# Products of the unit matrix issued in TensorE's long waits, into the bank that is written next

## Chip, cores and metric

One core of one Trainium2 chip. The metric is the device time of one execution in microseconds; lower is better.

## What is computed

Three blocks follow one another on an activation of 1024 tokens x 1024 channels, all in float32. Cut to what shapes the kernel:

```python
def first_block(x, ...):        # an even layer, an odd layer, rmsnorm
    # even: p = rmsnorm(h, g) @ w_in; an RWKV recurrence over tokens (8 heads of 64) and a banded
    #       softmax attention (8 heads) side by side; both gated; h + concat(y_a, y_b) @ w_out
    # odd:  p = rmsnorm(h, g) @ w_in; spatial gating: per 128 tokens and group, sg_w @ layernorm(v);
    #       h + (y * silu(gate)) @ w_out
def second_block(x, ...):       # one norm, one wide projection, three branches, merged
    # sliding-window attention with sinks, a 31-tap conv with layernorm, differential attention;
    # each branch through its w_o and a sigmoid merge gate; the sum @ w_out
def third_block(x, p, ...):
    # x = layer_norm(x); stick-breaking attention and a multiscale pool; @ w_out; layer_norm
    # h = square(relu(x @ w_up)) @ w_down; layer_norm;  x + (p @ w_ple) * sigmoid(x @ w_ple_gate); layer_norm
def step(state, inp):           # the recurrence inside the even layer
    r_t, w_t, k_t, v_t, a_t, b_t = inp
    sa = jnp.einsum('bhvk,bhk->bhv', state, a_t)
    state = state * w_t[:, :, None, :] + sa[..., None] * b_t[:, :, None, :] + v_t[..., None] * k_t[:, :, None, :]
    return state, jnp.einsum('bhvk,bhk->bhv', state, r_t)
```

## The kernel before

Each engine has one program, written out by hand in its final order; nothing is scheduled or reordered by a tool. The engines meet only through semaphores: `done(name)` gives the semaphore and the count at which a named step is finished, and an engine waits for it before it issues what needs it. So TensorE works through one fixed list, and whatever stands behind a waiting product waits too.

The results of products go to the eight PSUM banks. A ring (`Banks`) hands them out in turn. `open` takes the next bank, and `free` names the step that emptied it the last time round, which the program waits for first; the waits for the operands come behind that one.

The stages, in order: the first norm (`begin`); the RWKV branch (`pe_rwkv`) paced step by step against the banded attention (`pe_band`), 280 rounds of one against 192 of the other; the even layer's gate and output (`pe_even`); the odd layer (`pe_odd`); the projections of the second block, with head sums `hn` for its q and k norms, and the window attention (`pe_window`); the joins, the differential attention, the merge (`pe_merged`); the third block's attention (`pe_stick`), its output product (`pe_outp`), the MLP (`pe_mlp`) and the last gate.

The RWKV branch runs over four pairs of heads (c = 0 to 3). After the projections come transposes of v (`v_tr`), then four groups of 2 x 128 tokens. In `pe_factor` a group's triangular inverse is built by doubling: for i = 1 to 5 a product `ym` (four of 128x128), one `f` and one `g`, each emptied by VectorE or ScalarE before the next can start. Ahead of the first `ym` VectorE masks the scores and forms `Fm` and `Gm` (L2321 to L2332). The state steps of the group before (`pe_chunks`) and the band's products are woven between. At the end of a head pair VectorE normalises y in a row of 128x1024 operations (up to L2312), and then TensorE transposes it (`y_tr`).

At the end of a layer the tiles of 128 tokens are normalised one after another, and TensorE transposes each for the next stage (`pe_rms_tile`, `pe_ln_tile`, tile `tr`). `follow` issues a tile's transposes a few tiles of products later, so that the last tiles have no products left to stand between them. In the third block GpSimd ends each tile's norm (L3115).

`ident` is the 128x128 unit matrix in float32, made at the start. A float32 product leaves two records in the profile (one for each of its two passes), a product of float32r operands or a transpose leaves one.

Of the kernel before, what the change touches and what calls it, by code (L numbers as in the profile page):

```python
# [13 lines left out]
P = 128  # L14
# [154 lines left out]
def build(nc, T, out):  # L169
    ctx = ExitStack()  # L170
    with ctx:
# [15 lines left out]
        ident = sb("ident", [P, P])  # L187
# [82 lines left out]
        E = V = S = G = Y = Dry()  # L270
# [50 lines left out]
        def by4(b):  # L321
            return b.rearrange("p (b m n) -> p b m n", b=4, m=2)
# [7 lines left out]
        def gn(b):  # L330
# [2 lines left out]
        idb = ident[:, :].unsqueeze(1).to_broadcast([P, 4, P])  # L333
        handed = [(A[:, 768:1024], SIG[:, 256:512], by4(CS), by4(EX)),
                  (SIG[:, 512:768], SIG[:, 768:1024], by4(WS0[:, 3072:4096]), by4(WS1[:, 3072:4096]))]
        SM, SV = STAT[:, 48:64], STAT[:, 64:80]
        w_rw, w_band = slot(WS0, KD, 3 * P), slot(WS1, KD, 3 * P)
        w_lora = slot(WS0, KD, P, 3072)
# [150 lines left out]
                                                            4864)  # L489


        def pe_product_T(st, R_, name, wv, src, kt, c0, *waits):
            for half in range(2):
                b = R_.open(st.name, *name, half)
                pe.wait_ge(*R_.free(st.name, *name, half))
                for w in waits:
                    pe.wait_ge(*w)
                for k in range(kt):
                    mm = E.matmul(b[:, :], wv[:, k, c0:c0 + P], src[:, k, half * HALF:(half + 1) * HALF],  # L499
                                  start=k == 0, stop=k == kt - 1)  # L500
                mm.then_inc(*st.pe.mark(st.name, *name, half))
                yield
# [11 lines left out]
        def pe_transposes(st, R_, name, srcs, *waits):  # L514
            b = R_.open(st.name, *name)
            pe.wait_ge(*R_.free(st.name, *name))
            pe.wait_ge(*done("consts"))
            for w in waits:
                pe.wait_ge(*w)
            for i, s in enumerate(srcs):  # L520
                mm = E.transpose(b[:, i * P:(i + 1) * P], s, ident[:, :])  # L521
            mm.then_inc(*st.pe.mark(st.name, *name))

        def pe_split(st, R_, name, n, kt, left, right, *waits):
            b = R_.open(st.name, *name)
            pe.wait_ge(*R_.free(st.name, *name))
            for w in waits:
                pe.wait_ge(*w)
            ks = range(kt) if isinstance(kt, int) else kt
            for k in ks:  # L530
                (lh, ll), (rh, rl) = left(k), right(k)
                E.matmul(b[:, 0:n], lh, rh, start=k == ks[0], stop=False)  # L532
                E.matmul(b[:, 0:n], lh, rl, start=False, stop=False)  # L533
                mm = E.matmul(b[:, 0:n], ll, rh, start=False, stop=k == ks[-1])  # L534
            mm.then_inc(*st.pe.mark(st.name, *name))
# [42 lines left out]
        def pe_rwkv():  # L578
            after(pe, begin)
            run(pe_product_T(rw, for_rw, ("lora",), w_lora, XT, KD, 0, done("rwkv", "w_lora")))  # L580
            for c in range(4):
# [3 lines left out]
                for hf in range(2):  # L585
                    sl = slice(hf * HALF, (hf + 1) * HALF)
                    for lo, what in ((0, "sig"), (64, "a")):
                        b = for_rw.open("rwkv", what, c, hf)
                        pe.wait_ge(*for_rw.free("rwkv", what, c, hf))
                        pe.wait_ge(*done("rwkv", "lora_ready"))  # L590
                        pe.wait_ge(*done("rwkv", "w_lora2"))
                        E.matmul(b[:, :], W2[lo:lo + 64, c * P:(c + 1) * P], LT[lo:lo + 64, sl], start=True,
                                 stop=True).then_inc(*rw.pe.mark("rwkv", what, c, hf))
# [44 lines left out]
        def pe_factor(c, grp):  # L638
# [20 lines left out]
            for i in range(1, 6):  # L659
                yield  # L660
                b = for_rw.open("rwkv", "ym", c, grp, i)
                pe.wait_ge(*for_rw.free("rwkv", "ym", c, grp, i))
                pe.wait_ge(*done("rwkv", "al", c, grp, i))
                pe.wait_ge(*done("rwkv", "fg", c, grp, i - 1))
                for q in range(4):
# [37 lines left out]
            for i in range(2):  # L703
                t = 2 * grp + i
# [106 lines left out]
        def pe_odd():  # L811
# [11 lines left out]
            def mixed(t):  # L823
                yield from nothing(4)
                for hf in range(2):
                    b = every.open("odd", "mix", t, hf)
                    pe.wait_ge(*every.free("odd", "mix", t, hf))
                    pe.wait_ge(*done("odd", "vn", t))
                    pe.wait_ge(*done("odd", "sgt"))
                    for g in range(4):  # L830
                        gg = hf * 4 + g
                        mm = E.matmul(b[:, g * P:(g + 1) * P], VN_O[:, t, gg * P:(gg + 1) * P], SGT[:, gg, :],
                                      start=True, stop=True)
                    mm.then_inc(*odd.pe.mark("odd", "mix", t, hf))
                yield
# [34 lines left out]
        def pe_head_sums(st, areas, order, k):  # L870

            name = order[k]
            b = every.open(st.name, "hn", *name)
            pe.wait_ge(*every.free(st.name, "hn", *name))
            pe.wait_ge(*done(st.name, "sq", *name))
            E.matmul(b[:, :], head_ones[:, :], areas[k % 2][1], start=True, stop=True).then_inc(
                *st.pe.mark(st.name, "hn", *name))
# [2696 lines left out]
```

## Time and profile before

| | |
|---|---|
| median of 3 runs | 4776.83 us (4765.28 to 4786.88) |
| the profiled execution | 4775.21 us, span 4773.1 us, mean granted TensorE clock 0.931 |
| TensorE busy | 4285.7 us (90% of the span), 21360 records |
| VectorE, ScalarE, GpSimd busy | 1861.4, 1319.7, 1121.0 us |
| DMA | 35 GB/s over the span, q1 at 10.7% of its engines |

All times are from the start of the span. A busy share is that of an engine's own instructions; the granted clock of a stretch is the mean of two levels, 2.4 GHz (1.0) and 1.2 GHz (0.5). An "idle before" is the time in which the engine stood still just ahead of a row, with the instruction that ended it.

### The profile page before, as it was taken

What the parts mean: (1) busy time and instruction counts of PE and PEld (TensorE: products, weight loads), DVE (VectorE), ACT (ScalarE), POOL (GpSimd) and SP (SyncE); (2) the same over time, 40 slices, a digit from 0 to 9 for tenths busy, and PEclk for the clock granted to TensorE, in tenths of its full rate; (3) what the DMA queues carried; (4) which work ended last, traced back from release to release, by engine and by line L of the source; (5) the groups of instructions that cost most, each with busy time, mean ns of one, the idle gap of its engine ahead of it and who ended that gap; (6) DMA issues with size and microseconds to landing.
All of it is one profiled execution on the core that took longest, in us unless ns stands there. A gap on an engine that the chain in (4) does not pass through costs nothing.

```text
span 4773.1 us, 50138 instructions
## 1 busy us (share of the span) xinstructions
PE 4285.7 (90%) x21360; PEld 3309.7 (69%) x21360; DVE 1861.4 (39%) x3046; ACT 1319.7 (28%) x2333; POOL 1121.0 (23%) x579
## 2 busy tenths in 40 slices
PE   8888888888978999988799997998998989999988
PEld 4775756757548889766667775776447768888877
DVE  2444425434222312685520358222137332333243
ACT  3222222222112322444321236211137222111223
POOL 1101101101111143674322210223000043232343
PEclk9999898898989999998899988999998889999989
DMA  2101000000021111210011110121100011111110
GB/s 79 27 1 28 1 15 14 1 15 1 5 98 36 36 53 36 80 40 18 18 36 40 49 36 1 51 73 47 35 18 1 27 62 44 53 45 53 45 53 36
DMA packets 155582, 168.08 MB, mean 35 GB/s; under 512 B 8032, under 2 KB 137952, under 8 KB 155360
## 3 DMA queue, kind: packets, MB, share of 16 engines
q1 hardware_dynamic: 155360, 164.89, 10.7%
q8 instruction: 168, 2.75, 0.2%
q14 instruction: 54, 0.44, 0.0%
HBM read 156.48 MB, written 8.39 MB: 35 GB/s over the span
## 4 chain that ended last, share of the span: by engine, by line
PE 41%; DVE 5%; ACT 2%; POOL 1%; issue 1%; DMA 0%; POOLq 0%; ACTq 0%; DVEq 0%
PE bank L532 9%; PE bank L533 9%; PE bank L534 9%; PE bank L510 4%; PE bank L499 3%; PE bank L977 2%; PE bank L521 1%; PE bank L995 1%; PE bank L1142 1%; PE bank L1118 1%; POOL H L3113 0%; POOL H L3115 0%; PE bank L1025 0%; DVE BIG L2743 0%; DVE BIG L2806 0%
## 5 line engine op out<-in xcount | busy, mean ns | idle before, releaser
L532 PE MATMUL bank<-XT_r,W_r 128*128 128x512 f32 x1712 | 701.2, 410 | 11.0 <-POOL BIG_r L3216 8.2
L533 PE MATMUL bank<-BIG_r,W_r 128*128 128x512 f32 x1712 | 677.5, 396 | 0.0
L499 PE MATMUL bank<-XT,W 128*128 128x512 f32 x1312 | 584.1, 603 | 20.5 <-DMA W<-w_in_e 17.8
L499 PEld LDWEIGHTS bank<-XT,W 128*128 128x128 f32 x1312 | 250.9, 194 | 330.1 <-issue 321.0
L534 PE MATMUL bank<-XT_r,W_r 128*128 128x512 f32 x1200 | 475.5, 396 | 0.0
L532 PE MATMUL bank<-W_r,BIG_r 128*128 128x256 f32 (+1 forms) x1280 | 419.1, 327 | 9.0 <-DVE MIX_r L2472 4.5
L3068 POOL TENSOR_TENSOR W_r<-W,W_r 128x2048 fp32r<-128x2048 f32 (+1 forms) x64 | 260.8, 4075 | 612.2 <-ACT W_r L1263 612.2
L532 PEld LDWEIGHTS bank<-XT_r,W_r 128*128 128x128 f32 x1712 | 329.4, 192 | 91.2 <-issue 21.3
L533 PEld LDWEIGHTS bank<-BIG_r,W_r 128*128 128x128 f32 x1712 | 329.1, 192 | 78.0 <-issue 11.3
L534 PE MATMUL bank<-W_r,BIG_r 128*128 128x256 f32 (+1 forms) x1152 | 381.2, 331 | 0.0
L1253 ACT ACTIVATE BIG<-bank 128x512 f32<-128x512 f32 (+3 forms) x246 | 130.0, 537 | 494.6 <-PE bank L499 153.6
L534 PEld LDWEIGHTS bank<-XT_r,W_r 128*128 128x128 f32 x1200 | 231.4, 193 | 50.0
L532 PEld LDWEIGHTS bank<-W_r,BIG_r 128*128 128x128 f32 x1280 | 244.5, 191 | 31.0 <-ACT BIG_r L1596 4.9
L521 PE MATMUL bank<-ident,BIG 128*128 128x128 f32 x688 | 133.7, 344 | 136.5 <-ACT BIG L1253 51.3
L3216 POOL TENSOR_TENSOR BIG_r<-MIX,W_r 128x2048 fp32r<-128x2048 f32 x36 | 165.4, 4596 | 329.8 <-ACT W_r L1927 329.8
L534 PEld LDWEIGHTS bank<-W_r,BIG_r 128*128 128x128 f32 x1152 | 219.6, 191 | 20.0
L521 PEld LDWEIGHTS bank<-ident,BIG 128*128 128x128 f32 x688 | 100.1, 177 | 177.6 <-ACT BIG L1253 70.8
L533 PE MATMUL bank<-W_r,BIG_r 128*128 128x256 f32 x768 | 218.2, 284 | 0.0
L534 PE MATMUL bank<-W_r,MIX_r 128*128 128x256 f32 x768 | 218.2, 284 | 0.0
L3113 POOL TENSOR_TENSOR H<-H,BIG 128x1024 f32<-128x1024 f32 x32 | 75.8, 2367 | 600.9 <-ACT H L1370 600.9
L2870 DVE TENSOR_TENSOR H<-H,bank 128x512 f32<-128x512 f32 x240 | 161.7, 686 | 121.0 <-PE bank L534 121.0
L534 PE MATMUL bank<-XT_r,BIG_r 128*128 128x512 f32 x512 | 200.1, 391 | 0.0
(391 smaller groups left out, 7912.3 us busy)
## 6 DMA issues: line engine op xcount, KB each, us to landing
W<-w_in SPq DMA_DIRECT2D x22, 1024.0 KB, 5.3
MIX<-w_up SPq DMA_DIRECT2D x16, 1024.0 KB, 5.4
MIX<-w_down SPq DMA_DIRECT2D x16, 1024.0 KB, 4.8
W<-w_in_e SPq DMA_DIRECT2D x26, 512.0 KB, 6.5
W<-w_in_o SPq DMA_DIRECT2D x12, 1024.0 KB, 5.1
W<-w_in SPq DMA_DIRECT2D x17, 512.0 KB, 4.0
H<-x SPq DMA_DIRECT2D x16, 512.0 KB, 7.7
W<-w_out SPq DMA_DIRECT2D x8, 1024.0 KB, 5.2
```

Source lines behind the costliest of these rows:

```text
L499: mm = E.matmul(b[:, :], wv[:, k, c0:c0 + P], src[:, k, half * HALF:(half + 1) * HALF], start=k == 0, stop=k == kt - 1)
L510: mm = E.matmul(b[:, 0:n], src[:, k, t * P:(t + 1) * P], wv[:, k, c0:c0 + n], start=k == 0, stop=k == kt - 1)
L521: mm = E.transpose(b[:, i * P:(i + 1) * P], s, ident[:, :])
L532: E.matmul(b[:, 0:n], lh, rh, start=k == ks[0], stop=False)
L533: E.matmul(b[:, 0:n], lh, rl, start=False, stop=False)
L534: mm = E.matmul(b[:, 0:n], ll, rh, start=False, stop=k == ks[-1])
L977: mm = E.matmul(b[:, :], wo[:, k, :], half_of(Yb[:, k, :], half), start=k == 0, stop=k == 3)
L1253: S.activation(dst, R_.bank(st.name, *name)[:, 0:width], ACT.Copy, scale=scale).then_inc(*st.act.mark("ev", st.name, *name))
L2870: V.tensor_tensor(h, h, b, ALU.add).then_inc(*ff.dve.mark("ev", "mlp", "down", n, t, c0))
L3068: G.tensor_tensor(WLO[k % 2][:, 0:n], WSTAGE[k % 2][:, 0:n], WHI[k % 2][:, 0:n], ALU.subtract).then_inc(*s_split.mark("split", k))
L3113: G.tensor_tensor(x, x, ROWS[:, 0:D], ALU.mult).then_inc(*st.pool.mark())
L3216: G.tensor_tensor(WL[k % 2][:, :], STAGE[k % 2], WH[k % 2][:, :], ALU.subtract).then_inc(*st.pool.mark(st.name, "split", k))
```

## The change

A table `KEEP_UP` names 52 places in TensorE's program, each by the bank that it opens, and gives a number of products, 699 in all. At such a place `pe_keep_up` issues that many products of the unit matrix with itself, 128x128 in float32, into columns 0 to 127 of the bank that has just been opened. It stands behind the wait for the bank and ahead of the waits for the operands. The real product starts with `start=True` and overwrites what they left. The products signal nothing, no other engine's program changes, and no wait is added.

The places: ahead of the first gate product on the low-rank path (`sig`), the transposes of v (4) and of y (4), and the first `ym` of 15 of the 16 groups, all in the RWKV branch; the even gate; tiles at the ends of the even, odd, merge, output and MLP stages (18); three `mix` products and the first output product of the odd layer; four head sums; and the MLP's first product.

```diff
--- before.py
+++ after.py
@@ -333,6 +333,16 @@
         idb = ident[:, :].unsqueeze(1).to_broadcast([P, 4, P])
         handed = [(A[:, 768:1024], SIG[:, 256:512], by4(CS), by4(EX)),
                   (SIG[:, 512:768], SIG[:, 768:1024], by4(WS0[:, 3072:4096]), by4(WS1[:, 3072:4096]))]
+        KEEP_UP = {("rwkv", "sig", 0, 0): 18, ("even", "gate", 0, 0): 48, ("odd", "out", 0, 0): 15,
+                   ("mlp", "up", 0, 0, 0): 28, ("odd", "mix", 4, 0): 8, ("odd", "mix", 5, 0): 12, ("odd", "mix", 6, 0): 7,
+                   ("window", "hn", "q", 1, 0): 21, ("window", "hn", "q", 2, 1): 15, ("window", "hn", "q", 3, 1): 4,
+                   ("window", "hn", "k", 1, 1): 7}
+        KEEP_UP.update({("rwkv", "v_tr", c, 0): 14 for c in range(4)})
+        KEEP_UP.update({("rwkv", "y_tr", c, 0): n for c, n in enumerate((10, 38, 38, 42))})
+        KEEP_UP.update({("rwkv", "ym", c, grp, 1): 8 for c in range(4) for grp in range(4) if c or grp})
+        for st_, ts in (("even", {5: 15, 6: 15, 7: 5}), ("odd", {2: 7, 3: 4, 4: 15}), ("merged", {4: 17, 5: 9, 6: 9, 7: 9}),
+                        ("outp", {5: 22, 6: 14, 7: 14}), ("mlp", {0: 7, 4: 12, 5: 10, 6: 14, 7: 14})):
+            KEEP_UP.update({(st_, "tr", t, 0): n for t, n in ts.items()})
         SM, SV = STAT[:, 48:64], STAT[:, 64:80]
         w_rw, w_band = slot(WS0, KD, 3 * P), slot(WS1, KD, 3 * P)
         w_lora = slot(WS0, KD, P, 3072)
@@ -489,10 +499,16 @@
                                                             4864)
 
 
+        def pe_keep_up(b, *name):
+
+            for _ in range(KEEP_UP.get(name, 0)):
+                E.matmul(b[:, 0:P], ident[:, :], ident[:, :], start=True, stop=True)
+
         def pe_product_T(st, R_, name, wv, src, kt, c0, *waits):
             for half in range(2):
                 b = R_.open(st.name, *name, half)
                 pe.wait_ge(*R_.free(st.name, *name, half))
+                pe_keep_up(b, st.name, *name, half)
                 for w in waits:
                     pe.wait_ge(*w)
                 for k in range(kt):
@@ -515,6 +531,7 @@
             b = R_.open(st.name, *name)
             pe.wait_ge(*R_.free(st.name, *name))
             pe.wait_ge(*done("consts"))
+            pe_keep_up(b, st.name, *name)
             for w in waits:
                 pe.wait_ge(*w)
             for i, s in enumerate(srcs):
@@ -524,6 +541,7 @@
         def pe_split(st, R_, name, n, kt, left, right, *waits):
             b = R_.open(st.name, *name)
             pe.wait_ge(*R_.free(st.name, *name))
+            pe_keep_up(b, st.name, *name)
             for w in waits:
                 pe.wait_ge(*w)
             ks = range(kt) if isinstance(kt, int) else kt
@@ -587,6 +605,7 @@
                     for lo, what in ((0, "sig"), (64, "a")):
                         b = for_rw.open("rwkv", what, c, hf)
                         pe.wait_ge(*for_rw.free("rwkv", what, c, hf))
+                        pe_keep_up(b, "rwkv", what, c, hf)
                         pe.wait_ge(*done("rwkv", "lora_ready"))
                         pe.wait_ge(*done("rwkv", "w_lora2"))
                         E.matmul(b[:, :], W2[lo:lo + 64, c * P:(c + 1) * P], LT[lo:lo + 64, sl], start=True,
@@ -660,6 +679,7 @@
                 yield
                 b = for_rw.open("rwkv", "ym", c, grp, i)
                 pe.wait_ge(*for_rw.free("rwkv", "ym", c, grp, i))
+                pe_keep_up(b, "rwkv", "ym", c, grp, i)
                 pe.wait_ge(*done("rwkv", "al", c, grp, i))
                 pe.wait_ge(*done("rwkv", "fg", c, grp, i - 1))
                 for q in range(4):
@@ -825,6 +845,7 @@
                 for hf in range(2):
                     b = every.open("odd", "mix", t, hf)
                     pe.wait_ge(*every.free("odd", "mix", t, hf))
+                    pe_keep_up(b, "odd", "mix", t, hf)
                     pe.wait_ge(*done("odd", "vn", t))
                     pe.wait_ge(*done("odd", "sgt"))
                     for g in range(4):
@@ -872,6 +893,7 @@
             name = order[k]
             b = every.open(st.name, "hn", *name)
             pe.wait_ge(*every.free(st.name, "hn", *name))
+            pe_keep_up(b, st.name, "hn", *name)
             pe.wait_ge(*done(st.name, "sq", *name))
             E.matmul(b[:, :], head_ones[:, :], areas[k % 2][1], start=True, stop=True).then_inc(
                 *st.pe.mark(st.name, "hn", *name))
```

TensorE's list at the end of head pair c = 1 of the RWKV branch, before. L742/L743 and L769 are the last state step and band scores, L521 the transposes (`ident,MIX` is `y_tr`), L592 the low-rank products of the next head pair:

```order
512 L769 MATMUL bank<-H 128x128
513 L521 MATMUL bank<-ident,H 128x128
514 L521 MATMUL bank<-ident,MIX 128x128 x8
515 L592 MATMUL bank<-BIG 128x512 x4
516 L499 MATMUL bank<-XT,W 128x512 x8
```

The same place now; L505 is the product in `pe_keep_up`:

```order
523 L789 MATMUL bank<-H 128x128
524 L538 MATMUL bank<-ident,H 128x128
525 L505 MATMUL bank<-ident 128x128 x38
526 L538 MATMUL bank<-ident,MIX 128x128 x8
527 L611 MATMUL bank<-BIG 128x512 x4
528 L515 MATMUL bank<-XT,W 128x512 x8
```

Thirty-eight products stand between the band's last transpose and `y_tr`; the order of the rest is as it was.

TensorE's list ahead of a group's first `ym` (c = 2, third group). L725 and L729 are state products (L745 and L749 now), L667 is `ym` (L687 now), L734 and L736 (L754 and L756) the next state step, L675 (L695) the `f` product. Before:

```order
629 L725 MATMUL bank<-BIG 128x128
630 L729 MATMUL bank<-BIG 128x128
631 L667 MATMUL bank<-BIG 128x128 x4
632 L521 MATMUL bank<-ident,H 128x128 x5
633 L734 MATMUL bank<-BIG 128x128
```

And now:

```order
644 L745 MATMUL bank<-BIG 128x128
645 L749 MATMUL bank<-BIG 128x128
646 L505 MATMUL bank<-ident 128x128 x8
647 L687 MATMUL bank<-BIG 128x128 x4
648 L538 MATMUL bank<-ident,H 128x128 x5
649 L754 MATMUL bank<-BIG 128x128
```

Eight products stand ahead of `ym`, behind the state products.

## Rows read from the trace of the kernel before

**Rows 1.** The profile's page: span, busy time, granted clock in 40 slices

```profile
span 4773.1 us, 50138 instructions
...
PE 4285.7 (90%) x21360; PEld 3309.7 (69%) x21360; DVE 1861.4 (39%) x3046; ACT 1319.7 (28%) x2333; POOL 1121.0 (23%) x579
...
PEclk9999898898989999998899988999998889999989
```

**Rows 2.** 70 half-rate stretches (window, length, busy by engine, clock, DMA)

```profile
22.50:29.30 6.80, 5.82 (x24) 4.71 (x24) 4.08 (x10) 3.85 (x7) 0.00 (x0) 0.50 1.04 257
...
sum 664.10, PE 489.31 PEld 389.08 DVE 325.68 ACT 227.78 POOL 146.12; mean PE 6.99 PEld 5.56 DVE 4.65 ACT 3.25 POOL 2.09
```

**Rows 3.** Two like steps of the RWKV chain as windows

```profile
808.72:822.65 13.93, 13.93 (x57) 12.43 (x57) 4.40 (x10) 2.28 (x5) 1.55 (x2) 0.50 0.00 1
829.00:837.19 8.19, 7.21 (x51) 6.00 (x51) 4.87 (x11) 2.56 (x6) 1.27 (x1) 1.00 0.00 0
```

**Rows 4.** TensorE's waits (us in total, times, longest)

```profile
PE bank L667 <- DVE BIG L2332: 40.4, 15, 3.9
```

**Rows 5.** TensorE in order of time (start, us, instructions, [idle before <-releaser])

```profile
277.84 1.13 PE L667 MATMUL bank<-BIG 128*128 128x128 f32 x8 [1.02 <-DVE BIG L2332]
...
669.79 5.30 PE L510 MATMUL bank<-W,XT 128*128 128x128 f32 x46
...
674.92 0.39 PE L725 MATMUL bank<-BIG 128*128 128x128 f32 x2
...
690.37 1.97 PE L521 MATMUL bank<-ident,MIX 128*128 128x128 f32 x8 [11.08 <-DVE MIX L2312]
...
750.83 3.65 PE L521 MATMUL bank<-ident,BIG 128*128 128x128 f32 x16 [4.08 <-DVE BIG L2222]
...
862.79 1.62 PE L667 MATMUL bank<-BIG 128*128 128x128 f32 x6 [3.09 <-DVE BIG L2332]
...
1352.47 23.12 PE L499 MATMUL bank<-XT,W 128*128 128x512 f32 x48 [14.63 <-DMA W<-w_in_e]
```

**Rows 6.** 128x128 products back to back at half rate, TensorE in order of time

```profile
810.59 1.92 PE L682 MATMUL bank<-BIG 128*128 128x128 f32 x8
...
812.29 1.81 PE L783 MATMUL bank<-H 128*128 128x64 f32 x8
```

**Rows 7.** TensorE's ladder of transposes at the output stage's end

```profile
3871.70 1.94 PE L521 MATMUL bank<-ident,H 128*128 128x128 f32 x8 [6.44 <-DVE STAT L2151]
3883.98 1.94 PE L521 MATMUL bank<-ident,H 128*128 128x128 f32 x8 [4.26 <-POOL H L3115]
3894.09 0.76 PE L532 MATMUL bank<-XT_r,W_r 128*128 128x512 f32 x1 [8.17 <-POOL BIG_r L3216]
```

**Rows 8.** Half-rate stretches of the RWKV stage after filled waits, 21 windows: sum

```profile
sum 155.90, PE 148.63 PEld 126.82 DVE 54.14 ACT 38.24 POOL 19.99; mean PE 7.08 PEld 6.04 DVE 2.58 ACT 1.82 POOL 0.95
```

**Rows 9.** Half-rate stretches of the later stages after filled waits, 11 windows: sum

```profile
sum 54.10, PE 49.88 PEld 40.18 DVE 22.72 ACT 15.18 POOL 21.40; mean PE 4.53 PEld 3.65 DVE 2.07 ACT 1.38 POOL 1.95
```

**Rows 10.** Six of these stretches (452.9, 690.4, 1012.7, 1090.8, 1352.5, 3894.1): sum

```profile
sum 38.20, PE 36.54 PEld 26.00 DVE 5.72 ACT 9.79 POOL 8.98; mean PE 6.09 PEld 4.33 DVE 0.95 ACT 1.63 POOL 1.50
```

**Rows 11.** Four of them, after ladders (1525.0, 3300.3, 3894.1, 4623.6): sum

```profile
sum 28.20, PE 24.03 PEld 20.11 DVE 5.97 ACT 5.98 POOL 10.93; mean PE 6.01 PEld 5.03 DVE 1.49 ACT 1.49 POOL 2.73
```

**Rows 12.** Two waits and the clock behind them

```profile
368.87 1.10 PE L521 MATMUL bank<-ident,MIX 128*128 128x128 f32 x8 [3.01 <-DVE MIX L2312]
...
490.08 1.19 PE L667 MATMUL bank<-BIG 128*128 128x128 f32 x4 [1.66 <-DVE BIG L2332]
...
365.00:375.00 10.00, 6.16 (x25) 2.63 (x24) 4.44 (x5) 4.90 (x7) 0.00 (x0) 1.00 0.09 15
490.10:496.90 6.80, 6.80 (x29) 6.35 (x30) 2.43 (x7) 1.47 (x4) 1.27 (x1) 0.50 0.01 2
```

**Rows 13.** TensorE's first transposes

```profile
15.24 1.97 PE L521 MATMUL bank<-ident,BIG 128*128 128x128 f32 x8 [0.55 <-ACT BIG L1310]
20.36 1.06 PE L521 MATMUL bank<-ident,BIG 128*128 128x128 f32 x8 [0.90 <-DVE STAT L2048]
```

## Prediction

> **What bounds the kernel now.** I read the page first [rows 1]. TensorE is busy 90% of the span, no other engine above 39%, and the granted clock dips in many of the 40 slices. TensorE sets the time, then, and it is slowed in two ways: it waits, and for a while after some waits it runs at half rate. The second view is a table of the stretches in which the granted clock is 0.50, the lower level of 1.2 GHz. There are 70, of 664.1 us together, with TensorE busy for 489.3 us of them [rows 2]. The rest of the span runs at 1.0, 2.4 GHz.
>
> What does a half-rate stretch cost? The third view sets two like steps of the RWKV chain side by side, from one `f` product to the next [rows 3]. At 1.0 the step took 8.19 us for 51 records, at 0.50 it took 13.93 us for 57. By the columns of their products the two hold nearly the same work. So the slow one pays 5.74 us, 0.41 of its busy time. Nothing hid it: VectorE's and TensorE's parts alternate, and each product that lasts longer moves the whole chain. If I scale by records (8.19 x 57 / 51 = 9.15), it pays 4.8 us, or 0.34. If everything merely halved, it would be 0.50. I take 0.41, and keep the other two for the range.
>
> The waits that go before are in the waits view and in the order of time: the first `ym` of a group behind VectorE's masks (L2332, 40.4 us in 15 waits) [rows 4], `y_tr` 11.08 us, `v_tr` 4.08, the even gate 14.63 behind its weights' DMA [rows 5], the output stage's ladder 6.44, 4.26 and 8.17 [rows 7].
>
> **The change: what the products cost.** A 128x128 float32 product is two records. Back to back at full clock, 46 records took 674.92 - 669.79 = 5.13 us, so 0.112 each and 0.223 us for a product [rows 5]. At half rate 8 records took 812.29 - 810.59 = 1.70 us, 0.425 us for a product [rows 6]. So 699 products are 156 us of TensorE at full clock, and whether they cost anything is a question of room. The waits have it: 38 products before `y_tr` are 8.5 us in a wait of 11.08; 14 before `v_tr` 3.1 in 4.08; 8 before `ym` 1.8 in 3.09; 48 before the even gate 10.7 in 14.63 [rows 5]; 22 and 14 in the ladder 4.9 and 3.1 in 6.44 and 4.26; 28 before the MLP 6.3 in 8.17 [rows 7]. All end about 1 us or more before the operands come. I find one place without room, the `ym` that waited 1.02 us (1.8 us of products, 0.8 us late) [rows 5]. The wait that covers them belongs to VectorE, ScalarE, GpSimd or a DMA, and none of these has a new instruction or a new wait. The bank is waited for first, but it was free at or before the end of the previous product nearly everywhere, since a ring of four or eight banks lies between. Queued behind the products stand only the product that waits anyway and what follows it. If the cover were gone, the cost would be the 156 us.
>
> **What they give.** The change can touch only the falls of the clock that follow one of its 52 places. I took each half-rate stretch of that kind, from the moment when the operands came to its end. What lies earlier is waiting, which a faster clock does not shorten. In the RWKV stage these are 21 stretches with 148.6 us of busy time [rows 8], later 11 with 49.9 us [rows 9]. Together 198.5 us, and at 0.41 that is 82 us if every such fall goes away; 67 us at 0.34, 99 at 0.50.
>
> Not all of them will go. The products end early, and the rest of the wait stays idle. The trace has a fall straight after a wait of 1.66 us, and none after one of 3.01 us [rows 12], so the length of a wait alone does not decide, and a rest of 1 us may or may not be harmless. Two classes follow. Where more than about 2 us stay idle I count the fall as kept: two `y_tr` (11.08 - 8.5 = 2.6), the even gate (3.9), the MLP's first product (1.9), and the two `ym` whose waits are longest (3.9 us in [rows 4], less 1.8). By the same windows these six hold 36.5 us of busy time [rows 10], so 15 us. Of the other 67 us I take one in five as kept, since the chain behind `ym` has idle time of its own in every step (8.19 less 7.21 us busy in the fast one [rows 3]): 13 us. And where the clock is already low as the products begin, they run at 0.425 and come late: 14 before `v_tr` take 6.0 us for 4.08, 1.9 late. One or two such places and the short `ym` make 3 us.
>
> Sum: 82 - 15 - 13 - 3 = 51 us. From the profiled execution's 4775.2 us that is 4724. The median of the three runs is 1.6 us above this execution, so 4726.
>
> The 38 half-rate stretches that remain (window and differential attention, the stick-breaking rounds, the band's steps) have no products before them and stay as they are.
>
> **A rule against the change.** TensorE's first instructions are transposes, products against the unit matrix. Eight took 1.97 us at 15.24 and, with nothing but transposes in between, 1.06 us at 20.36 [rows 13]: the clock rose while only they ran. The Trainium skill (TensorE: Matmul & The Clock Gate, Part 4: PE-mode transpose) says the full clock does not engage for transpose-mode, which is not counted as busy in the same way. Here the trace disagrees. By that rule the ladders, where only transposes stand between the filled waits, would keep their falls.
>
> **Rivals.**
> *Falls kept in the ladders.* If what stands between the waits does too little, the ladders of the even, merge, output and MLP stages keep their falls. Their part is 24.0 us of busy time [rows 11], 10 us at 0.41; 5.9 of it (the MLP's first product) is already counted as kept. So 7 us less gain, 4733. The first transposes speak against it. It lies inside my range and goes with the forecast.
>
> *Half of the falls stay.* The idle rests of 1.0 to 1.5 us are enough together with the chain's own idle time. The gain is 82 / 2 = 41, less the 15 that are kept in any case and some 6 us of late operands: 20 us, 4756. The fall after 1.66 us speaks for it, the full clock after 3.01 us against.
>
> *The products don't hold the clock at all, and make operands' consumers late: slower.* The unit matrix with itself is mostly zeros, and no row shows a product of just that kind. If the clock falls where it did, the rest of the products runs at 0.425. All of them at that rate would overrun their waits by 5.1 us at each of two `y_tr` (38 x 0.425 - 11.08), 5.8 at the gate (20.4 - 14.63), 3.7 at the MLP (11.9 - 8.17), 1.9 at a `v_tr`, 0.3 at a `ym` [rows 5, 7], some 80 us over the 52 places. About the first 2 us of each wait still pass at full clock, which takes off nearly 0.9 us a place: 35 us remain, 4811. It decides once the lateness passes what the prevented falls give back. The first transposes speak against it, since they too are products with the unit matrix.
>
> *Every fall goes:* 82 us, 4694.
>
> **How the numbers follow.** Forecast with its ladder variant, 4705 to 4751: 0.64. Half or more stay, 4751 to 4775: 0.20. Nearly all go, below 4705: 0.10. Products that don't hold the clock: 0.05. No effect either way: 0.01. The range leaves out the slow rival, the best of the full gain at 0.50, and the weakest part of the second: 4694 to 4759. From no change a measurement of this kernel tells about 0.5%, 24 us. Gains under 24 us have most of the second case: faster 0.79, same 0.16, slower 0.05.
>
> **What would show it.** TensorE's records rise by 1398 to 22758. The sum of half-rate stretches falls from 664 us to under 350, and the mean granted clock rises from 0.931 to about 0.97. Before `y_tr` and `ym` a block of products ends 1 us or more before the operand's row, and the idle time there shrinks to the rest. The steps behind `ym` take some 8 us in place of 14. Wrong would be: half-rate stretches that begin inside the blocks of products, or rows that now follow such a block without idle time, at twice the price; or waits of TensorE that grow elsewhere by what the RWKV chain gained.

## The result and the profile after

The changed kernel took 4727.11 us (median of 4 runs, 4725.53 to 4728.78) against 4777.45 us (4765.28 to 4786.88) before: a ratio of 0.9896, 95% interval 0.9873 to 0.9919. It is faster by 50 us, 1.0%. The forecast was 4726.0.

The page of the kernel after, its lines on the span, on TensorE and on the granted clock, which answer to [rows 1]:

```profile
span 4723.6 us, 52912 instructions
...
PE 4374.3 (93%) x22758; PEld 3410.2 (72%) x22758; DVE 1859.8 (39%) x3046; ACT 1317.7 (28%) x2333; POOL 1120.0 (24%) x579
...
PEclk9998999999999999998899988999998899999999
```

TensorE has 1398 more records and is busy for 88.6 us more, and yet the span is shorter. The mean granted clock rose from 0.931 to 0.959. (The record of the clock begins with its first rise, at 19.0 us before and 24.0 us after; what lies ahead of it is counted as full.) The half-rate stretches as windows, after (the first two of 55 and their sum; columns as in [rows 2]):

```profile
303.90:324.40 20.50, 18.18 (x67) 14.25 (x65) 5.00 (x15) 3.15 (x8) 0.00 (x0) 0.50 0.00 1
430.20:437.00 6.80, 5.79 (x30) 5.49 (x32) 3.48 (x7) 2.24 (x6) 0.22 (x1) 0.50 0.00 0
...
sum 390.70, PE 332.89 PEld 258.71 DVE 175.58 ACT 136.59 POOL 64.20; mean PE 6.05 PEld 4.70 DVE 3.19 ACT 2.48 POOL 1.17
```

Seventy stretches of 664.1 us [rows 2] became 55 of 390.7 us. The product itself and TensorE's two great waits of [rows 4, 7], now; the first line is from the groups, the two others from the waits:

```profile
L505 PE MATMUL bank<-ident 128*128 128x128 f32 x1398 | 169.6, 280 | 2.8 <-DVE BIG_r L2185 1.7 <-ACT MIX L1275 0.9
```

```profile
PE bank L538 <- POOL H L3137: 21.7, 16, 1.9
...
PE bank L687 <- DVE BIG L2354: 13.5, 13, 2.2
```

`ym`'s wait for the masks fell from 40.4 us with 3.9 at most to 13.5 with 2.2 at most. What the waits look like from inside is in TensorE's order of time. First `y_tr` of c = 1 (in [rows 5] the row with 11.08 us of idle time), then one step of the chain at c = 2 (as in [rows 3]), then `y_tr` of c = 3 and the even gate:

```profile
664.49 8.65 PE L505 MATMUL bank<-ident 128*128 128x128 f32 x76
675.72 1.78 PE L538 MATMUL bank<-ident,MIX 128*128 128x128 f32 x8 [2.58 <-DVE MIX L2334]
...
833.73 2.05 PE L505 MATMUL bank<-ident 128*128 128x128 f32 x16
836.95 1.13 PE L687 MATMUL bank<-BIG 128*128 128x128 f32 x8 [1.17 <-DVE BIG L2354]
...
839.19 1.16 PE L695 MATMUL bank<-BIG 128*128 128x128 f32 x8
...
847.01 1.13 PE L695 MATMUL bank<-BIG 128*128 128x128 f32 x8
...
1284.32 10.86 PE L505 MATMUL bank<-ident 128*128 128x128 f32 x84
1296.96 1.09 PE L538 MATMUL bank<-ident,MIX 128*128 128x128 f32 x8 [1.78 <-DVE MIX L2334]
1298.99 10.96 PE L505 MATMUL bank<-ident 128*128 128x128 f32 x96 [0.94 <-ACT MIX L1275]
1313.09 5.40 PE L515 MATMUL bank<-XT,W 128*128 128x512 f32 x8 [3.15 <-DMA W<-w_in_e]
```

The reader is to see three things. The 76 records before `y_tr` end 2.58 us ahead of the operand, and behind that rest the eight transposes take 1.78 us: this fall stayed. The 16 before `ym` end 1.17 us ahead, `ym` takes 1.13 us, and the step from one `f` to the next takes 847.01 - 839.19 = 7.82 us. And before the gate 3.15 us stay idle, behind which the clock fell too.

Where the time came from, by stages. Each ends with the first record of the product named, and half-rate us stand in brackets; both are worked out from the traces. The rows together are the whole span. The last three columns belong to the last experiments.

| stage up to | before | after | spare bank | more covered | both |
|---|---|---|---|---|---|
| `v_tr` c = 0 | 129.6 (15.0) | 126.6 (0) | 127.2 (6.8) | 127.3 (6.8) | 127.9 (6.8) |
| `v_tr` c = 1 | 308.6 (43.0) | 298.7 (20.5) | 298.5 (20.5) | 291.7 (3.4) | 292.5 (3.4) |
| `v_tr` c = 2 | 312.6 (66.2) | 310.3 (44.4) | 309.7 (44.4) | 296.8 (10.2) | 297.7 (13.7) |
| `v_tr` c = 3 | 321.7 (84.0) | 301.0 (23.9) | 300.9 (23.9) | 300.4 (23.9) | 300.4 (23.9) |
| even gate | 279.9 (80.7) | 276.6 (37.5) | 279.5 (44.4) | 270.8 (23.9) | 271.6 (23.9) |
| odd layer's first transposes | 176.1 (19.0) | 175.3 (6.8) | 172.2 (0) | 172.2 (0) | 172.4 (0) |
| odd layer's first output product | 301.5 (14.8) | 299.3 (3.4) | 300.2 (6.8) | 297.8 (0) | 299.2 (3.4) |
| second block's projections | 122.3 (8.3) | 118.3 (0) | 118.7 (0) | 118.2 (0) | 118.4 (0) |
| window attention's first scores (projections, head sums) | 192.3 (10.2) | 192.5 (3.4) | 192.5 (0.2) | 192.5 (0) | 192.6 (2.1) |
| joins (the window attention) | 235.4 (70.6) | 235.2 (70.6) | 220.5 (19.2) | 235.0 (70.6) | 215.8 (14.4) |
| third block's output product | 1366.4 (175.1) | 1366.7 (151.5) | 1366.5 (151.3) | 1369.9 (171.8) | 1365.8 (150.7) |
| MLP's first product | 147.7 (28.3) | 147.7 (6.6) | 148.0 (6.8) | 146.7 (6.7) | 146.8 (6.9) |
| last gate | 733.1 (26.5) | 729.6 (0.3) | 729.6 (0.4) | 729.7 (0) | 729.6 (0) |
| end | 146.0 (19.7) | 145.8 (19.6) | 145.8 (19.5) | 145.8 (18.8) | 145.9 (18.7) |

Up to the even gate the kernel before needs 1352.5 us and the changed one 1313.1: 39.4 of the 49.5 us by which the spans differ. All that follows gives 10.

### The profile page after: what moved, and what is told of

Its sections match the earlier page's. It is cut to its first block, busy times and chain, and to the rows that moved or that the text cites. A ratio compares the mean times of both kernels' runs of the same rounds, so it can differ in the third digit from the quotient of the medians.

```text
span 4723.6 us, 52912 instructions
## 1 busy us (share of the span) xinstructions
PE 4374.3 (93%) x22758; PEld 3410.2 (72%) x22758; DVE 1859.8 (39%) x3046; ACT 1317.7 (28%) x2333; POOL 1120.0 (24%) x579
## 4 chain that ended last, share of the span: by engine, by line
PE 42%; DVE 5%; ACT 2%; POOL 1%; issue 1%; DMA 0%; POOLq 0%; ACTq 0%; DVEq 0%
PE bank L550 9%; PE bank L551 9%; PE bank L552 9%; PE bank L526 4%; PE bank L515 4%; PE bank L999 2%; PE bank L1017 1%; PE bank L538 1%; PE bank L1140 1%; PE bank L1164 1%; POOL H L3135 0%; POOL H L3137 0%; PE bank L1047 0%; DVE BIG L2828 0%; DVE BIG L2765 0%
## 5 line engine op out<-in xcount | busy, mean ns | idle before, releaser
L515 PE MATMUL bank<-XT,W 128*128 128x512 f32 x1312 | 582.2, 602 | 10.2 <-DMA W<-w_in_e 6.5
L1275 ACT ACTIVATE BIG<-bank 128x512 f32<-128x512 f32 (+3 forms) x246 | 129.9, 536 | 489.9 <-PE bank L515 153.5
L550 PEld LDWEIGHTS bank<-W_r,BIG_r 128*128 128x128 f32 x1280 | 244.1, 191 | 27.3 <-issue 4.0
L551 PE MATMUL bank<-BIG_r 128*128 128x512 f32 x512 | 199.2, 389 | 0.0
```

Of the source, the lines that this page charges most:

```text
L1275: S.activation(dst, R_.bank(st.name, *name)[:, 0:width], ACT.Copy, scale=scale).then_inc(*st.act.mark("ev", st.name, *name))
```

## The experiments

Theory A in the expectations is the prediction's own: the products keep the clock up, and a fall costs 0.41 of TensorE's busy time in it, wherever it lies. The rivals stand beside it in each expectation. All kernels compute the whole output. The edits are to the changed kernel.

**Only the RWKV places.**

```diff
+        KEEP_UP = {k: n for k, n in KEEP_UP.items() if k[0] == "rwkv"}
```

> Only the 24 places of the RWKV branch keep their products (322 of 699). Theory A (the gain is the higher clock behind the waits, in proportion to the busy time of the half-rate stretches that vanish): the changed kernel left TensorE's `even gate` 39.4 us earlier and gave 50.3 us in all, so this version gains 38 to 40 us, 4738, about 0.992 of the kernel before. Theory B (a cost of about 1 us for the first product after every long wait, whatever the clock, which any product in the wait takes away): 24 of 52 places give 23 us, 4754, 0.995.

Measured: 4732.16 us, ratio 0.9911 (0.9898 to 0.9924), a gain of 44 us with 322 of the 699 products. Theory B of the expectation (a cost of 1 us for each long wait, whatever the clock) had 23 us.

**Only the later places.**

```diff
+        KEEP_UP = {k: n for k, n in KEEP_UP.items() if k[0] != "rwkv"}
```

> Only the 28 places outside the RWKV branch keep their products (377 of 699). Theory A (clock): 10 to 12 us of gain, 4766, 0.9977, since most of these places stand in ladders of transposes that wait for another engine anyway. Theory B (a cost of each long wait): 28 of 52 places give 27 us, 4750, 0.994. By either theory the gains of this version and of the RWKV-only one add up to 50 us.

Measured: 4772.61 us (4764.54 to 4781.29), ratio 0.9991 (0.9983 to 1.0), a gain of 4 us with 377 products. The gain goes neither by the number of products nor by that of waits (theory B had 27 us here), and both parts together make 48 of the 50 us. In this version's profile the stages behind the even gate without the window attention give 10.3 us, in the changed kernel 10.0, but the window attention, which the edit doesn't touch, took 6.0 us more than before. Much of the half-rate time that vanished in the later stages gave nothing, and the output stage's ladder shows why. TensorE's order of time in the changed kernel, where [rows 7] were:

```profile
3825.29 1.09 PE L538 MATMUL bank<-ident,H 128*128 128x128 f32 x8 [1.45 <-POOL H L3137]
3826.22 3.29 PE L505 MATMUL bank<-ident 128*128 128x128 f32 x28
3831.43 1.09 PE L538 MATMUL bank<-ident,H 128*128 128x128 f32 x8 [1.93 <-POOL H L3137]
3832.36 3.29 PE L505 MATMUL bank<-ident 128*128 128x128 f32 x28
3837.58 1.09 PE L538 MATMUL bank<-ident,H 128*128 128x128 f32 x8 [1.93 <-POOL H L3137]
3840.34 8.01 PE L505 MATMUL bank<-ident 128*128 128x128 f32 x56 [1.67 <-DVE BIG_r L2185]
3848.11 0.48 PE L550 MATMUL bank<-XT_r,W_r 128*128 128x512 f32 x1
```

The transposes take 1.09 us in place of 1.94, so the clock stayed up. But a tile follows the one before it after 6.14 and 6.15 us, and before the two steps from 3871.70 to 3883.98 [rows 7] took 12.28 us, 6.14 each on average. The tiles come at the pace at which their norm is made, and a slow transpose between two waits costs nothing. That is the stage in which the half-rate time fell by 21.7 us and the span not at all. Before the MLP's first product the block began at 3840.34 behind 1.67 us of idle time, in which the clock had just fallen (at 3840.1). So its 56 records took 8.01 us (at 0.112 each 6.3), and the product follows it without a rest, 10.53 us after the start of the last tile's transposes in place of 10.11 [rows 7]: late by 0.4 us or more.

**Transposes in place of products.** Two for each product, so that the number of records stays.

```diff
-            for _ in range(KEEP_UP.get(name, 0)):
-                E.matmul(b[:, 0:P], ident[:, :], ident[:, :], start=True, stop=True)
+            for _ in range(2 * KEEP_UP.get(name, 0)):
+                E.transpose(b[:, 0:P], ident[:, :], ident[:, :])
```

> The same 52 places, but each product of the unit matrix is replaced by two transposes of it, so that the number of records and their time stay. If transposes hold the clock as products do, as TensorE's first transposes suggested: 4727, 0.990, half-rate stretches of about 390 us together. If transposes are not counted as work (the rule of the Trainium skill, TensorE: Matmul & The Clock Gate, Part 4: PE-mode transpose): the falls come back, 664 us at half rate, no gain, and late operands on top, 4777 to 4811, 1.000 to 1.007.

Measured: 4721.51 us, ratio 0.9887 (0.9874 to 0.99), with 56 half-rate stretches of 390.8 us and a mean clock of 0.959. The block before `y_tr` of c = 1, TensorE in order of time:

```profile
660.53 8.46 PE L505 MATMUL bank<-ident 128*128 128x128 f32 x76
671.76 1.30 PE L538 MATMUL bank<-ident,MIX 128*128 128x128 f32 x8 [2.77 <-DVE MIX L2334]
```

76 transposes ran at the full pace, 0.11 us each, and the half-rate sum is the same to 0.1 us. That closeness is chance, since many of the stretches lie elsewhere, but the clock, the sum and the time agree: transposes hold the clock as well as products do. The Trainium skill's rule in TensorE: Matmul & The Clock Gate, Part 4: PE-mode transpose (the full clock does not engage for them) does not hold for this kernel.

**Twice the products.**

```diff
+        KEEP_UP = {k: 2 * n for k, n in KEEP_UP.items()}
```

> Twice as many products at each place (1398). By the waits of the changed kernel's trace, each place less 2n x 0.223 us, the products overrun their waits by 88 us in all at full clock. If lateness counts in full: 4727 + 88, less up to 10 us since the last falls behind filled waits vanish: 4805 to 4815, 1.006 to 1.008. If the chains of the other engines have slack that absorbs it: under 4770, faster than the kernel before or no different.

Measured: 4789.16 us, ratio 1.0029 (1.0019 to 1.0038). Now the blocks outlast their waits. TensorE in order of time at the same place:

```profile
675.96 17.14 PE L506 MATMUL bank<-ident 128*128 128x128 f32 x152
692.93 1.04 PE L539 MATMUL bank<-ident,MIX 128*128 128x128 f32 x8
```

152 records in 17.14 us are 0.113 each, all at full clock, and `y_tr` follows without a rest, 16.97 us after the block's start. In the changed kernel it came 11.23 us after it, so it is 5.7 us late. The kernel pays 62 us over the changed one for 699 products more, 156 us of work. The expectation had 78 to 88 us for lateness counted in full: most of it counts, and some is absorbed. At `y_tr` the covered part costs nothing and the uncovered part its length.

**The products behind the waits for the operands.** `pe_keep_up` moved below the waits at all seven call sites; one of them:

```diff
-            pe_keep_up(b, st.name, *name)
             for w in waits:
                 pe.wait_ge(*w)
+            pe_keep_up(b, st.name, *name)
```

> The same 699 products at the same places, but issued behind the waits for the operands in place of ahead of them, so that nothing covers them and the waits stay idle. Theory A: the falls come as in the kernel before, and 699 x 0.223 us are added, less what the ladders of transposes absorb: 4900 to 4935, 1.026 to 1.033. If this version were near the changed kernel's time, the covering would not matter and the gain would come from the products as such.

Measured: 4874.47 us, ratio 1.0204 (1.0191 to 1.0217), 97 us above before. TensorE in order of time:

```profile
710.96 10.99 PE L505 MATMUL bank<-ident 128*128 128x128 f32 x76 [11.07 <-DVE MIX L2334]
721.79 1.04 PE L538 MATMUL bank<-ident,MIX 128*128 128x128 f32 x8
```

The wait is back at 11.07 us, the clock falls in it, and the block lies wholly behind it. So the products' gain is a matter of place: the same 699 give 50 us ahead of the wait and take 97 behind it. That is less than their 156 us at full clock. It is also less than the 123 to 158 us that the expectation had. Part came back where a block let the clock rise before its real product (`y_tr` above: 1.04 us, [rows 5]: 1.97), and the half-rate sum is 548.1 us in place of 664.1. How much the time to spare in the ladders took off isn't measured.

**Larger numbers at 37 of the places**, so that about 0.5 us of each wait stay (`y_tr` of c = 1 and 3 get 48, the even gate 60, nine `ym` 10 to 16, most tiles of the ladders 14 to 27):

```diff
+        KEEP_UP.update({('rwkv', 'sig', 0, 0): 22, ('rwkv', 'v_tr', 0, 0): 16, ('rwkv', 'ym', 0, 1, 1): 11,
...
```

> The changed kernel's own places, but at 37 of them the number of products is raised so that about 0.5 us of the wait stays idle in place of 1 to 3 us (y_tr 48 for 38, the even gate 60 for 48, most ym 11 for 8). Theory A, with my two classes of falls that are kept because of the idle rest: most of the dozen falls behind filled waits go, 10 to 15 us less, 4713, 0.987. Rival (the rest is harmless, and those that remain have other causes such as unfilled waits near by): 4727 or some us more from late operands.

Measured: 4724.23 us, ratio 0.9892 (0.9877 to 0.9906), some 3 us better than the changed kernel, a difference within the scatter. The expectation had 10 to 15 us, and its rival none. At `y_tr` of c = 1 the fall is gone:

```profile
662.73 10.88 PE L517 MATMUL bank<-ident 128*128 128x128 f32 x96
673.96 1.09 PE L550 MATMUL bank<-ident,MIX 128*128 128x128 f32 x8 [0.35 <-DVE MIX L2346]
```

But the half-rate sum fell only to 380.1 us, though the falls that had stayed behind filled waits were 51 us long (the last view of after, below). What remains lies behind waits that have no products: the transposes `b_tr`, the band's transposes, and towards the even gate short waits of the state products. The stage up to the even gate took 282.7 us with 54.6 at half rate, in place of 276.6 with 37.5, the stage up to `v_tr` of c = 2 took 303.8 us with 27.3, in place of 310.3 with 44.4. That filling one wait better passes its fall on to the next is a guess that such numbers suggest and don't show: with the RWKV places unchanged, the run with the window attention (below) had 304.8 us with 30.7 and 278.7 with 44.4 in these two stages.

**The window attention's waits too**, 150 products at 14 places, into the bank that is written next:

```diff
+        KEEP_UP.update({('window', 'hn', 'q', 1, 1): 5, ('window', 'p_tr', 7, 1): 6, ('window', 'p_tr', 6, 1): 10,
...
```

> The changed kernel, and 150 more products at 14 waits of the window attention (its score and output transposes and one head sum), which the change leaves as they are. In the changed kernel's trace the half-rate stretches of that stage hold 64.9 us of TensorE's busy time. Theory A (half rate costs 0.41 of the busy time behind a wait, wherever TensorE then works): 27 us less than the changed kernel, 4700, 0.984. Rival (the waits of this stage end with the softmax chain of the other engines, so that a faster TensorE only waits longer): 4725, 0.989, with the same number of half-rate stretches gone.

Measured: 4749.14 us, ratio 0.994 (0.9924 to 0.9955), 22 us slower than the changed kernel, where theory A had 27 less and the rival 2 less. The stage went from 235.2 to 269.0 us, and its half-rate time only from 70.6 to 66.9. TensorE there, in the changed kernel and in this one:

```profile
2134.73 1.12 PE L538 MATMUL bank<-ident,BIG 128*128 128x128 f32 x4 [2.96 <-ACT BIG L1275]
...
2150.11 0.77 PE L538 MATMUL bank<-ident,BIG 128*128 128x128 f32 x4 [3.58 <-ACT BIG L1275]
```

```profile
2133.97 4.64 PE L510 MATMUL bank<-ident 128*128 128x128 f32 x20 [2.95 <-ACT BIG L1280]
2138.40 1.06 PE L543 MATMUL bank<-ident,BIG 128*128 128x128 f32 x4
...
2151.77 5.54 PE L510 MATMUL bank<-ident 128*128 128x128 f32 x26 [3.57 <-ACT BIG L1280]
2157.15 0.60 PE L543 MATMUL bank<-ident,BIG 128*128 128x128 f32 x4
```

The idle time of 2.96 and 3.58 us is as it was, and the products start behind it. The ring that these transposes use has a single bank, so what TensorE waits for here is the bank: ScalarE's copy (L1275) empties it, and until then nothing may be written there, products of no use either. They had no cover at all.

**Every wait over about 1.5 us**: the larger numbers, the window attention's places and 19 more (`b_tr`, the band's `p_tr`, the differential and the stick-breaking attention), 318 products at 33 new places.

> The raised numbers and 318 more products at 33 waits that had none: the window attention, and the longest waits of the band, of the second transposes of each head pair, and of the differential and stick-breaking attention. Theory A: 12 us for the raised numbers, 27 for the window attention and about 15 for the rest, 4673, 0.978. Rival (the attention stages wait for other engines' chains): 4715, 0.987.

Measured: 4744.38 us, ratio 0.9932 (0.9919 to 0.9944), with 37 half-rate stretches of 287.4 us and the mean clock at 0.970. The stages up to the even gate took 1281.3 us, 32 less than in the changed kernel; the window attention took 38 more, the differential attention 9 more (462.7 us for 453.5). In both, all new blocks but one head sum's start behind 1.9 to 4.4 us of idle time, as in the run before. Both theories of the expectation (4673, 4715) missed that. A higher mean clock is not a shorter time.

**The window attention's products into another bank.** The next bank of the joins' ring (two banks, `for_join`) is free during the window attention, once the step that emptied it last is done:

```diff
+        def pe_spare(*name):
+            if name in SPARE:
+                k = len(for_join.order)
+                pe.wait_ge(*done("ev", *for_join.order[k - 2]))
+                for _ in range(SPARE[name]):
+                    E.matmul(for_join.banks[k % 2][:, 0:P], ident[:, :], ident[:, :], start=True, stop=True)
...
+            pe_spare(st.name, *name)
             b = R_.open(st.name, *name)
             pe.wait_ge(*R_.free(st.name, *name))
```

> The changed kernel, and the window attention's products (139 at 12 transposes, 5 at a head sum) again, but now written into the bank that the first merge opens next, ahead of the wait for the transposes' own bank. In the run with these products in their own bank TensorE issued them only when that bank was free (3.1 to 3.8 us after the previous product), so they lay behind the wait. Theory A (clock, and cover decides the price): they now lie inside the wait, 27 us less than the changed kernel, 4700, 0.984. Rival (this stage is set by ScalarE's chain and the single bank, a faster TensorE waits longer): 4720 to 4727, 0.988 to 0.990.

Measured: 4698.89 us (4682.11 to 4711.82), ratio 0.9825 (0.9809 to 0.984), 28 us better than the changed kernel with nearly the same products that cost 22 us in their own bank. TensorE in order of time:

```profile
2137.41 2.50 PE L518 MATMUL bank<-ident 128*128 128x128 f32 x20
2140.44 0.66 PE L552 MATMUL bank<-ident,BIG 128*128 128x128 f32 x4 [0.53 <-ACT BIG L1289]
...
2149.50 3.12 PE L518 MATMUL bank<-ident 128*128 128x128 f32 x26
2153.26 0.66 PE L552 MATMUL bank<-ident,BIG 128*128 128x128 f32 x4 [0.63 <-ACT BIG L1289]
```

The blocks fill the wait that was idle, and the transposes behind them take 0.66 us in place of 1.12. In this profile the stage is 14.7 us shorter and its half-rate time 19.2 us in place of 70.6 (the table). The profiled execution was the slowest of the five (4711.8); where the others gained more, no trace shows.

**Larger numbers, and nine further waits that are for operands** (three `b_tr`, four `p_tr` of the band, its gate, the even output), with 22 products before the MLP's first product in place of 28. A head sum gets the 5 products that it had in the run before, a tenth new place:

```diff
...
+                        ('mlp', 'up', 0, 0, 0): 22, ('band', 'p_tr', 0, 7, 0): 8, ('band', 'p_tr', 1, 7, 0): 10,
+                        ('rwkv', 'b_tr', 1, 0): 12, ('band', 'p_tr', 2, 4, 0): 8, ('rwkv', 'b_tr', 2, 0): 12,
...
```

> The raised numbers, and products at nine further waits for operands in the RWKV branch, the band and the even layer (b_tr of three head pairs, four band transposes, a band gate, the even output), none at waits for a bank. In the run that filled all waits the stages up to the even gate took 1281 us, in the changed kernel 1313. Theory A: 30 to 35 us less than the changed kernel, 4694, 0.982. Rival (the 32 us were luck in where the falls lay): 4710 or more.

Measured: 4697.04 us (4694.96 to 4699.97), ratio 0.983 (0.9817 to 0.9844), 38 stretches of 338.4 us, 30 us better than the changed kernel, as theory A had it.

**Both together.**

> Both of the former together. If the gains are from separate stages they add up: 4727 - 33 - 27 = 4667, 0.977; if the window attention gives nothing: 4692, 0.982.

Measured: 4670.82 us (4659.23 to 4678.46), ratio 0.9773 (0.9758 to 0.9788). It is the best version, 107 us below before and 56 below the changed kernel: the 28 and 30 us of its two parts add up. Its page, and the sum of its 31 half-rate stretches as windows:

```profile
span 4676.6 us, 54437 instructions
...
PEclk9999999999999999999999998999997899999999
```

```profile
sum 270.20, PE 221.76 PEld 169.82 DVE 129.01 ACT 98.86 POOL 23.78; mean PE 7.15 PEld 5.48 DVE 4.16 ACT 3.19 POOL 0.77
```

## Why the prediction was right

**That the products hold the clock and lie under the waits: right, and shown.** The records rose to 22758, and behind most blocks the full clock stays. Placed behind the wait the same products cost 97 us, and twice the number costs 62 us over the changed kernel. The slow rival, that the products don't hold the clock, is out: the 76 records before `y_tr` took 8.65 us, 0.114 each, where 0.112 was forecast. (Its price was too high as well. If the first 2 us of a wait pass at full clock, some nine products of a long block take 0.223 us each in place of 0.425. That takes off 1.8 us a place, not 0.9, and by the same waits some 21 us of lateness remain, 4797 in place of 4811.) The rule on transposes is refuted by the run with transposes. In the rows on the first transposes the prediction read the clock off their durations; the record of the clock, which begins at 19.0 us, agrees with it.

**The room: less than the prediction said.** "All end about 1 us or more before the operands come", with one place without room, was wrong. By the same trace's waits 22 of the 52 blocks had less than that, among them two more `ym` with none, behind waits of 1.66 and 1.83 us. After, 29 blocks end 1 to 3.2 us ahead of the operands and 23 less than 1 us, three of these without any rest. It cost little: of the three, the `ym` of [rows 5] was forecast as 0.8 us late.

**The price of a fall, 0.41 of its busy time: right.** The two kernels issue the same real records in the same order, so each of the 32 stretches that the sum priced [rows 8, 9] can be followed from before to after by its records. In 21 of them nothing is left at half rate. They held 129.8 us of busy time and became 52.9 us shorter: 0.41. In the other 11, with 68.7 us of busy time, some or all of the fall stayed, and they gave 6.4 us where the full price is 28.3. So 22 us were kept, where 28 were forecast, and 59 us came in the priced stretches: 45 in the RWKV branch, 14 behind it.

**What became of the 59 us: the term that was too small.** The span fell by 49.5 us only, 39.4 up to the even gate and 10 behind it. So 10 us were lost outside the priced stretches, for which the sum had 3, the late operands. In the RWKV branch falls lay elsewhere than before: up to `v_tr` of c = 2 the priced stretches gave 10.0 us and the stage 2.3, up to `v_tr` of c = 3 they gave 16.5 and the stage 20.8, up to the even gate 7.0 and 3.3. Behind it the gain ran into the next wait: the head sums' stretches gave 2.5 us, and the stage with them became no shorter in any of the four versions in the table. That a slow transpose between two waits for a norm costs nothing is shown by the output stage, and the starts of the tiles in [rows 7], 12.28 us for two, could have told it. The sum had left such transposes out, since its stretches begin when the last operands came. What the later places give comes from dense products behind a wait, as in the stage up to the last gate (3.5 us) and up to the second block's projections (4.0).

**Falls kept, by place: half right.** Eleven falls of the trace after lie at filled places: three began ahead of a block, eight behind the filled wait. One of the eight, at 884.2, more likely belongs to the next wait, 1.73 us without products, since the filled one had left only 0.23 us. The eight as windows with their sum:

```profile
443.90:461.00 17.10, 14.85 (x60) 13.05 (x61) 4.26 (x9) 2.58 (x6) 3.77 (x3) 0.50 0.00 1
676.00:679.40 3.40, 3.40 (x14) 2.04 (x14) 0.69 (x1) 1.79 (x2) 0.00 (x0) 0.50 0.14 28
...
4577.50:4580.80 3.30, 3.08 (x15) 3.11 (x16) 0.69 (x1) 0.85 (x2) 1.77 (x1) 0.50 0.98 343
sum 51.00, PE 47.38 PEld 38.19 DVE 11.00 ACT 10.69 POOL 9.59; mean PE 5.92 PEld 4.77 DVE 1.37 ACT 1.34 POOL 1.20
```

By these, 47.4 us of busy time are 19 us at 0.41. Of the six that were named as kept, four were: the two longest `ym` (the first of these rows, with 2.2 us left idle, and one with 1.96 at 1054.8), `y_tr` of c = 1 (2.58 us left) and the gate (3.15). The two others were at half rate before their blocks began: the MLP's first product (at 3840.1), and `y_tr` of c = 2 (at 966.1), whose 76 records took 10.20 us and still ended in time. In the other direction, short falls at the ends of three ladders were not forecast (at 1488.3, 3256.4 and 4577.5). They came behind rests of 1.28, 1.63 and 1.95 us, each with a second wait of 0.99 to 1.78 us behind it. Other rests of up to 1.93 us brought no fall, so that no length of rest divides the two cleanly.

Two errors cancelled, then. The kept falls were over-counted by 6 us, and what is lost outside the priced stretches was put at 3 us where it is 10. That the median lies within 1 us of the forecast is luck in part.

**The half-rate sum and the clock: the step contradicted the sum.** Under 350 us and 0.97 were written, 390.7 and 0.959 came. The 38 stretches without products are 319 us of the 664 before, and 28 us of kept falls at 0.41 are 68 us of busy time: 387 us or more by the prediction's own terms. I had not added them. After, 64.6 us lie at filled places (the eight, and three that began ahead of a block), and the other 44 stretches are 326 us. That these "stay as they are" held nearly as a sum (38 of 319 us became 44 of 326), not by place. With `b_tr` and `p_tr` filled as well, the stages up to `v_tr` of c = 2 and up to the even gate had 10.2 and 23.9 us at half rate in place of 44.4 and 37.5, and the kernel gained 27 us over the one with the larger numbers alone.

**What stays open.** Why the clock falls behind one rest and not behind a like one isn't settled, nor why falls move in stages that an edit leaves alone. It shows in the scatter, too: in the run with the later places alone the window attention took 241.4 us with 80.9 at half rate in place of 235.4 with 70.6. So differences of 5 us between two kernels here are no more than suggested by their medians.

## What to carry to other kernels

Where the granted clock falls behind a wait of TensorE and a chain of dependent products follows, fill the wait with products of no use, counted from the wait's length and their pace, so that the block ends before the operand comes. Four fifths of what this change gained came from such chains, and nothing from ladders that run at another engine's pace. How much rest may stay isn't shown: leaving 0.5 us in place of 1 to 3 gave some 3 us, within the scatter. Ask first what the wait is for. A wait for an operand can be filled in the bank that is written next; a wait for the bank can't, and needs another bank that is free (here 28 us gained in place of 22 lost). And judge by the time, not by the clock: the kernel with a mean clock of 0.970 was slower than the one with 0.959.

## What was not expected of the hardware

Transposes of the unit matrix hold the granted clock as its products do: 0.959 on average with either, and 4721.5 us with the ones, 4727.1 with the others. And where the clock falls isn't fixed by the waits alone: in the stage up to `v_tr` of c = 2 three kernels with the same products there had 44.4, 44.4 and 30.7 us at half rate (the changed one, the window attention's products in the spare bank, and in their own bank).
